# A delta-rule recurrence on one core: the identity added at the eviction of W, X and Y copied out whole, four quadrants of the array in use

## What is computed

```python
def step(state, inp):                       # per head: 16 heads of 64 channels
    r_t, w_t, k_t, v_t, a_t, b_t = inp
    sa = jnp.einsum('bhvk,bhk->bhv', state, a_t)
    state = (state * w_t[:, :, None, :]
             + sa[:, :, :, None] * b_t[:, :, None, :]
             + v_t[:, :, :, None] * k_t[:, :, None, :])
    y_t = jnp.einsum('bhvk,bhk->bhv', state, r_t)
    return state, y_t
...
y_f = _wkv7_scan(r32, decay_h[0], k_dir[0], v32, -kk, b_dir[0], reverse=False)
y_b = _wkv7_scan(r32, decay_h[1], k_dir[1], v32, -kk, b_dir[1], reverse=True)
```

## Time and profile before

| | before |
|---|---|
| median of 3 executions | 2935.41 us |
| lowest and highest | 2929.65, 2935.97 us |
| span of the profiled execution | 2930.1 us |
| TensorE (PE) busy in it | 2793.3 us, 95% |
| VectorE (DVE) busy | 2161.7 us, 74% |
| ScalarE (ACT) busy | 1632.9 us, 56% |
| GpSimd (POOL) busy | 159.4 us, 5% |
| stretch with levels | about 173.6 to 445.6 us |

### The profile page before, as it was taken

One profiled execution on the slowest core, in us unless ns is written; L12 is line 12 of the kernel. 1 busy time (PEld: TensorE's weight loads), 2 busy tenths in 40 slices (PEclk: granted clock), 3 DMA queues, 4 the chain that ended last, 5 costly groups with the idle time before them and its releaser, 6 DMA issues.

```text
span 2930.1 us, 52775 instructions
## 1 busy us (share of the span) xinstructions
PE 2793.3 (95%) x21826; PEld 2485.1 (85%) x21826; DVE 2161.7 (74%) x2714; ACT 1632.9 (56%) x2317; POOL 159.4 (5%) x164
## 2 busy tenths in 40 slices
PE   6889999999999999999999999999999999999999
PEld 5877777778778999878787888999999979998998
DVE  7868875899996656689998666666666786668665
ACT  2445543788884444478888544445544824446443
POOL 0024430000000020100000000000000000000000
PEclk8989999999999999999999999999999999999999
DMA  7601124699995736179998413554455404544453
GB/s 318 237 2 46 60 74 155 232 354 350 356 354 192 273 132 243 44 288 353 356 357 339 187 58 118 185 186 147 155 186 187 157 12 177 186 159 142 148 185 129
DMA packets 78260, 572.73 MB, mean 195 GB/s; under 512 B 8802, under 2 KB 8930, under 8 KB 9186
## 3 DMA queue, kind: packets, MB, share of 16 engines
q1 hardware_dynamic: 76752, 558.93, 51.3%
q10 hardware_dynamic: 1298, 10.83, 0.9%
HBM read 568.67 MB, written 1.05 MB: 194 GB/s over the span
## 4 chain that ended last, share of the span: by engine, by line
PE 82%; DVE 12%; ACT 3%; DMA 1%; issue 1%; POOL 0%; DVEq 0%; SPq 0%; ACTq 0%; PEldq 0%
PE ps L1377 14%; PE ps L1299 13%; PE ps L1254 8%; PE ps L1398 7%; PE ps L863 5%; PE ps L865 5%; PE ps L864 5%; PE ps L1255 4%; DVE arena L2245 4%; DVE wl L2239 2%; DVE arena L2239 2%; PE ps L1497 1%; DMA ring<-in_stream 1%; PE ps L898 1%; PE ps L897 1%; PE ps L896 1%
## 5 line engine op out<-in xcount | busy, mean ns | idle before, releaser
L2239 DVE TENSOR_TENSOR wl<-ring,wh 128x1024 fp32r<-128x1024 f32 (+1 forms) x560 | 938.2, 1695 | 366.1 <-ACT wh L1636 345.6
L1636 ACT ACTIVATE wh<-ring 128x1024 fp32r<-128x1024 f32 (+1 forms) x560 | 789.5, 1432 | 454.4 <-PE ps L1255 209.6
L1254 PE MATMUL ps<-hx,wh 128*128 128x512 f32 x1024 | 362.4, 396 | 1.3 <-DVE wl L2239 1.3
L863 PE MATMUL ps<-hx,wh 128*128 128x256 f32 x1072 | 310.6, 290 | 22.5 <-DVE hx L2239 17.4
L864 PE MATMUL ps<-hx,wl 128*128 128x256 f32 x1072 | 306.5, 286 | 0.0
L865 PE MATMUL ps<-hx,wh 128*128 128x256 f32 x1072 | 306.3, 286 | 0.0
L1299 PE MATMUL ps<-hidh,wh 128*128 128x256 f32 x1024 | 290.4, 284 | 1.1 <-DVE hidl L2239 1.1
L1299 PE MATMUL ps<-hidl,wh 128*128 128x256 f32 x1024 | 289.8, 283 | 0.0
L1299 PE MATMUL ps<-hidh,wl 128*128 128x256 f32 x1024 | 289.7, 283 | 0.0
L1255 PE MATMUL ps<-hx,wl 128*128 128x256 f32 x1024 | 287.1, 280 | 0.0
L1633 ACT ACTIVATE arena<-arena 128x256 f32<-128x256 f32 (+7 forms) x420 | 207.2, 498 | 97.5 <-DVEq L2766 33.8
(11 more groups left out here) (286 smaller groups left out, 5662.0 us busy)
## 6 DMA issues: line engine op xcount, KB each, us to landing
ring<-in_stream SPq DMA_DIRECT2D x532, 1024.0 KB, 4.9
arena<-in_wcmp ACTq DMA_DIRECT2D x2, 2048.0 KB, 10.5
arena<-in_lora ACTq DMA_DIRECT2D x1, 2048.0 KB, 9.8
arena<-in_atm ACTq DMA_DIRECT2D x1, 1762.0 KB, 11.6
x<-in_xT ACTq DMA_DIRECT2D x1, 1024.0 KB
out<-x SPq DMA_DIRECT2D x1, 1024.0 KB, 3.9
arena<-in_rwm ACTq DMA_DIRECT2D x1, 736.0 KB, 12.8
cols<-in_cols ACTq DMA_DIRECT2D x1, 715.0 KB
```

Source lines behind the costliest of these rows:

```text
L863: mm(out, w[0], h[0], start=first, stop=False)
L1254: mm(o.rearrange("p (a s) -> p a s", a=2), w[0], hx[:, :, k, :], start=k == 0, stop=False, skip_group_check=True)
L1636: return nc.scalar.activation(out, in_, ACT.Copy)
L2239: return v.tensor_tensor(out, a, b, op)
```

## The change

**Algebra.** With Y = X', the sum X + Y'W is Y'(W + I), and Y + W'Y is (W + I)'Y. VectorE now evicts W with the identity added, as 256 columns for each `z`. The products of `level_xy` are then the new X and Y themselves, and ScalarE copies them out, 512 columns from two PSUM banks for each `z` (256 from one bank in level 5). The two engines have changed places in each level.

**Quadrants.** `y_half` says in which half Y and W lie: in their own at level 1, in the other one from level 2 on. X stays in its half. So the product for X and that for Y use different quadrants, and the four products of one `q` (X and Y, both halves) are written one behind another.

**PSUM.** W and X of a `z` share bank 2z, Y takes bank 2z + 1. W of level 1 therefore waits now until X of level 5 of the block before has been copied out.

**Order.** The evictions of the levels are moved on both engines, as is P0 on ScalarE. TensorE's order outside `level_xy`, and GpSimd's, are the same.

```diff
+        def y_half(lev, i):
+            return HALF[i if lev == 1 else 1 - i]
...
 def level_w(c, lev):                                  # TensorE
                         if lev == 1:
                             pe.wait_ge(ev("rw_x0"), c + 1)
+                            if c:
+                                pe.wait_ge(ev("rw_xy"), rw_at(c - 1, RW_LEVELS, z))
                         else:
                             pe.wait_ge(ev("rw_xy"), rw_at(c, lev - 1, z))
-                        t, A_ = ps[:, z, :], Al[(RW_LEVELS * c + lev - 1) % 3]
+                        t, A_ = ps[:, 2 * z, :], Al[(RW_LEVELS * c + lev - 1) % 3]
                         for q in range(4):
-                            for r in HALF:
-                                last = mm(t[r, 64 * q:64 * q + 64], A_[r, z, 64 * q:64 * q + 64], XY[c % 3][r, z, 0, 64 * q:64 * q + 64],
-                                          start=True, stop=True)
+                            a = slice(64 * q, 64 * q + 64)
+                            for i in (0, 1):
+                                last = mm(t[y_half(lev, i), a], A_[HALF[i], z, a], XY[c % 3][HALF[i], z, 0, a], start=True, stop=True)
...
 def level_xy(c, lev):                                 # TensorE
-                            for r in HALF:
-                                last = mm(t[r, a], XY[c % 3][r, z, 1, a], Wb[r, z, a], start=True, stop=True)
-                        if lev < RW_LEVELS:
-                            for q in range(4):
-                                a = slice(64 * q, 64 * q + 64)
-                                for r in HALF:
-                                    last = mm(t[r, 256 + 64 * q:320 + 64 * q], Wb[r, z, a], XY[c % 3][r, z, 1, a], start=True, stop=True)
+                            for i in (0, 1):
+                                h = y_half(lev, i)
+                                last = mm(ps[HALF[i], 2 * z, a], XY[c % 3][h, z, 1, a], Wb[h, z, a], start=True, stop=True)
+                            if lev < RW_LEVELS:
+                                for i in (0, 1):
+                                    h = y_half(lev, i)
+                                    last = mm(ps[HALF[1 - i], 2 * z + 1, a], Wb[h, z, a], XY[c % 3][h, z, 1, a], start=True, stop=True)
...
 def level(c, lev):                                    # ScalarE
-                        act.wait_ge(ev("rw_Wt"), rw_at(c, lev, z))
-                        copy(Wb[:, z, :], ps[:, z, 0:256]).then_inc(ev("rw_w"), 1)
+                        act.wait_ge(ev("rw_XYt"), rw_at(c, lev, z))
+                        if lev < RW_LEVELS:
+                            copy(XY[c % 3][:, z], ps[:, 2 * z:2 * z + 2, 0:256]).then_inc(ev("rw_xy"), 1)
+                        else:
+                            copy(XY[c % 3][:, z, 0, :], ps[:, 2 * z, 0:256]).then_inc(ev("rw_xy"), 1)
...
 def level(c, lev):                                    # VectorE
-                        dve.wait_ge(ev("rw_XYt"), rw_at(c, lev, z))
-                        a = XY[c % 3][:, z].rearrange("p x n -> p (x n)")[:, 0:512 if lev < RW_LEVELS else 256]
-                        tt(a, ps[:, 2 + z, 0:512 if lev < RW_LEVELS else 256], a, ADD).then_inc(ev("rw_xy"), 1)
+                        dve.wait_ge(ev("rw_Wt"), rw_at(c, lev, z))
+                        tt(Wb[:, z, :].rearrange("p (q t) -> p q t", q=4), ps[:, 2 * z, 0:256].rearrange("p (q t) -> p q t", q=4),
+                           rmask("eye")[:, None, :].to_broadcast([P, 4, 64]), ADD).then_inc(ev("rw_w"), 1)
```

More of the change, by code:

```diff
@@ L1758, in rwkv @@
                     on_e, on_f, on_c, on_p, on_g = e < C, 0 <= f < C, 0 <= c < C, 0 <= p < C, 0 <= g < C
+                    if on_p:
+                        solved("P", 0, p)
                     if on_c:
                         level(c, 1)
-                    if on_p:
-                        solved("P", 0, p)
                     if on_f:
@@ L1770, in rwkv @@
                         fn(cx, cx, ACT.Exp).then_inc(ev("rw_E"), 1)
-                    if on_c:
-                        level(c, 2)
                     if on_p:
@@ L1776, in rwkv @@
                         let(copy(Zv[c % 2], got("Zv", c)), "Zv", c)
+                        level(c, 2)
                     if on_p:
@@ L1787, in rwkv @@
                         let(copy(Vt[f % 3].rearrange("p j n -> p (j n)"), got("V", f)[:, 0:S]), "V", f)
-                    if on_c:
-                        level(c, 3)
                     if on_f:
@@ L1792, in rwkv @@
                             copy(Ast[f % 2][:, h].rearrange("p z j t -> p (z j t)"), got(f"sm{h}", f)[:, 0:256]).then_inc(ev("rw_A"), 1)
+                    if on_c:
+                        level(c, 3)
                     if on_g:
@@ L1818, in rwkv @@
                             let(copy(N6[f % 2][:, h].rearrange("p j t -> p (j t)"), got(f"n6{h}", f)[:, 0:P]), f"n6{h}", f)
-                    if on_c:
-                        level(c, 5)
                     if on_e:
@@ L1837, in rwkv @@
                         let(copy(ys, got("y", p)), "y", p)
+                    if on_c:
+                        level(c, 5)
                     if s == C:
@@ L2471, in rwkv @@
                     on_e, on_f, on_c, on_p, on_g = e < C, 0 <= f < C, 0 <= c < C, 0 <= p < C, 0 <= g < C
+                    if on_c:
+                        level(c, 1)
                     if on_f:
@@ L2486, in rwkv @@
                         modulation("ada1")
-                    if on_c:
-                        level(c, 1)
                     if on_p:
                         solved_r(p, 0)
+                    if on_c:
+                        level(c, 2)
                     if on_g:
@@ L2533, in rwkv @@
                         tt(X4, X4, rmask("eye")[:, None, None, :].to_broadcast([P, 2, 4, 64]), ADD).then_inc(ev("rw_x0"), 1)
+                    if on_c:
+                        level(c, 4)
                     if on_p:
@@ L2538, in rwkv @@
                             masked(Arb[f % 3], "rb", h, f, "incl")
-                    if on_c:
-                        level(c, 4)
                     if on_e:
```

3 lines of the change are left out of this document (removed).

## The result

The changed kernel takes 2914.5 us (median of 8 runs, 2900.2 to 2916.4), the kernel before on the same chip 2932.9: a ratio of 0.9935, interval 0.992 to 0.9949. Timed once more on the chip of the last experiments, it is 2905.1 against 2930.4: 0.9916 (0.9894 to 0.9938). So it is faster by 18 to 25 us. Forecast were 2919 and a range of 2903 to 2932, which holds both medians; but several terms of the sum were off, in opposite directions, as the profile shows.

The account below looks back on a forecast made before the run. Neither PE nor DVE alone was the bound: a step's first half is a DVE chain, its second mostly PE. Gains of 6 x 1.8 + 3 + 2.5 = 16.3 us from 2935.4 gave 2919 us, range 2903 to 2932.

Parts of the forecast that it names:

- step 0: First step, without U0: its 2.44 us wait before W of level 2 goes entirely, gaining about 3 us.
- steps 1 to 6: Six recurrence steps, each 34.3 instead of 36.1 us: 1.8 us less per step.
- step 7, to X of level 5: Last step, where DVE idles: PE's shorter products count, less some eviction waits, gaining 2.5 of 3.4 us.
- from there to the next stage: Stretch behind the last step's levels: no gain of its own in the sum; the next stage starts 16.3 us earlier.
- the walk: One step followed through PE, DVE and ACT in the new order: 34.3 instead of 36.1 us.
- the wait before W of level 2: PE's 0.97 us for late X and Y of level 1: mostly gone, but U0 then waits for R0; gain 0.4.
- the gain up to `sm`: First half of a step, on DVE: features at 12.6, `sm` at 12.75 us against 14.25, gain 1.5.
- R1 waits on ACT: P1's copy queues on ACT until 19.75, R1 starts at 19.9; half the gain is given back, 1.0 us left.
- four quadrants are no faster than two: Rival on X and Y products: a level stays at 2.0 us, total 2935 us; chance 0.13.
- The rival of a late ACT: A copy over two PSUM banks costs ACT 1.2 us, W of level 5 comes 1.55 later: 2947 us; chance 0.06.
- The rival of better meshing: DVE and PE mesh better, no waits at U0 and R1; halfway 3.5 us a step, 2907 us; chance 0.10.
- the price of the evictions: DVE's W plus identity costs 0.89 us a pair against 1.28 for X and Y: 1.55 us less DVE a step.

Follow-up runs that it names:

- changed, again: The changed kernel unchanged, in a second profiled execution (span 2904.5 us) and timed once more: 2905.1 us, ratio 0.9916 to the kernel before.
- P1 early: Changed kernel, but on ScalarE var's Exp and the squares of k moved behind BK and P1: 2911.7 us, ratio 0.9927 to the kernel before.
- busy_tail: Changed kernel plus overwritten filler products ahead of TensorE's waits at R and U from step 7 on and S and Z1 behind the last step: 2912.2 us.
- R0 early: Changed kernel, but on VectorE R0 is evicted directly behind the scans, ahead of what follows from them: 2903.3 us, ratio 0.9898 to the kernel before.
- the kernel in pairs: Changed kernel, but Y and W stay in their own half, so X and Y use the same two quadrants: 2921.5 us, ratio 0.9967 to the kernel before.
- the kernel before, again: The kernel before, unchanged, run once more for a second profile: 2945.5 us in one execution.

## Why the prediction was right, and where it was not

**The whole.** By stretches, from W of level 1 of step 0 to the stage behind the recurrence, against the profile of before:

| stretch, us | before | changed | changed, again | forecast gain | gain, changed and again |
|---|---|---|---|---|---|
| step 0 | 32.5 | 23.6 | 23.6 | 3 | 8.9 |
| steps 1 to 6 | 213.4 | 199.3 | 193.6 | 10.8 | 14.1, 19.8 |
| step 7, to X of level 5 | 25.1 | 26.1 | 23.4 | 2.5 | -1.0, 1.7 |
| from there to the next stage | 37.2 | 42.4 | 41.4 | 0 | -5.2, -4.2 |

It comes to 16.9 and 26.2 us, against 16.3. So the closeness to the first result is partly luck: steps 0 to 6 gained more than was forecast, and low clock, with stalls, took it back: 4.2 us behind the recurrence in both executions, and in the first 5.6 more in the steps, 2.7 in step 7 and 1.0 behind it. The tail's part is not shown to be the change's doing: the kernel before has 37.2 and 42.4 there in its two profiles, and other kernels with the change have 38.6 ("P1 early") to 42.8 (`busy_tail`).

**Right: the mechanisms of the walk.** Four quadrants do a level in 1.0 us (forecast 1.09); the wait before W of level 2 is gone, and U0 waits for R0 in its place; the gain up to `sm` is fixed by DVE (R0 early); R1 waits on ACT, whose queue holds P1 (P1 early), and gives back part. The wait of W of level 1 for X of level 5 costs nothing. But P1, forecast to come after a wait of about 1 us, hardly waits (without the block it starts only 0.15 earlier).

**The rivals.** That four quadrants are no faster than two is out: both halves of X write one bank, both of Y another, and a pair of X and one of Y together take the 58 ns that one pair took before. The Trainium skill, "TensorEngine Tiling (Array Packing)", section "Gotcha 1: PSUM Pressure", says that different row tiles cannot access the same PSUM bank simultaneously; in this pattern the trace shows nothing of it. That rival was also priced too high, 2935 with W of level 5 at 26.8: the kernel in pairs, which has just these products, has it at 26.15 and takes 2921.5. The rival of a late ACT is out: the pair of copies over two banks took 1.09, where it needed 1.8 to decide. The rival of better meshing, given 0.10, had the size: "some 3.5 a step" and 2907, where 3.2 and, in the second timing, 2905.1 were measured. Its mechanism did not come true, since it put the waits at U0 and R1 at nothing and they are there (0.80 and 1.34); what made the step shorter is the next point.

**Mis-sized: the price of the evictions.** The walk took 0.89 for a pair of W from a pair at the end of a wait. Queued behind other work a pair takes 0.74 (298.12, 302.21), and five of them are 0.75 less. A single eviction is about as long in both places (0.42 and 0.41): at 310.16 the second begins 0.47 after the first, since it still waits for PE, and in the queue 0.33 after. So 0.89 held a wait that the new place does not have. The block of 2048 columns, with 3.06 the dearest single term, took 2.41 here. That is more than scatter: the block at this place took 3.06 or 3.07 in steps 2 to 6 of both profiles of the kernel before, and 2.40 to 2.42 in steps 2 to 6 of "changed, again" and in steps 4 to 6 of the first profile of the changed kernel (2.90 and 2.52 in steps 2 and 3, which have low clock). Over all of the recurrence its mean went only from 2.73 to 2.60 (busy us and mean ns of one, before and then changed), since the step's other block went from 2.70 to 2.80. In step 7 and behind it, where GpSimd is idle, each block takes 2.34 or 2.35 in both kernels. Why the same instruction takes longer elsewhere was not tested. In all, DVE is busy 3.4 us less in a step, and the walk had 1.55.

```profile
L2245 DVE SCALAR_TENSOR_TENSOR ring<-ring,small 128x2048 f32<-128x2048 f32 x14 | 38.2, 2730 | 0.9 <-DVE under L2242 0.3 <-DVE spare L2245 0.3
```

```profile
L2250 DVE SCALAR_TENSOR_TENSOR ring<-ring,small 128x2048 f32<-128x2048 f32 x14 | 36.4, 2599 | 0.3 <-DVE spare L2250 0.3
```

Both lie on DVE's chain to P1, which comes at 16.2 and not 17.6: three pairs (0.45) and the block (0.65) are 1.1 of these 1.4 us. The remaining 0.3 I can't assign. The step is shorter than forecast by 1.4 too, 32.9 and not 34.3, but not by this alone. At W of level 5 only 1.0 of it is left (23.8 against 24.75). Another 0.4 comes behind it, where the walk said that nothing changes: `ka` and `kr` took 2.37 until the next W in the kernel before (310.51 to 312.88) and take 1.99 in "changed, again" (323.71 to 325.70).

```profile
310.51 2.45 PE L1235 MATMUL ps<-arena,under 64*128 64x128 f32 x32
```

```profile
323.71 2.06 PE L1238 MATMUL ps<-arena,under 64*128 64x128 f32 x32
```

**Wrong: step 0.** The forecast of 3 came from the wait of 2.44 us alone. What it did not see are the records right behind it: Zv at 180.52 took 3.19 us, against 2.00 in the step from 276.78, and X of level 2 1.12 for 16 records, against 0.68. The window of that stretch of the kernel before comes first (12 us at 0.72), then the whole step 0 of the changed kernel, at 1.00:

```profile
178.00:190.00 12.00, 9.71 (x146) 8.95 (x146) 7.23 (x13) 4.13 (x9) 0.00 (x0) 0.72 0.01 2
```

```profile
172.59:196.20 23.61, 21.05 (x612) 18.08 (x611) 19.18 (x38) 14.58 (x33) 11.33 (x14) 1.00 0.02 4
```

The same 612 records take 28.2 us of PE before and 21.1 after, of which the quadrants explain 3.6 (in pairs it is 24.6). A wait was costed by its length, without the slower records that follow it. The kernel in pairs has 25.7 for step 0 and clock 1.00, so hands and order bring 6.8 of the 8.9 us. Both profiles of the kernel before have the wait of 2.44 and a clock of 0.89 in step 0, and all eleven of kernels with DVE's new order have 1.00 there, so this gain is no chance of one execution. Step 1 has some of it too, since the kernel before has low clock there (34.6 us at 0.95, in "changed, again" 29.35 at 1.00).

**Wrong: the clock in the other steps.** Nothing in the forecast spoke of it, since the earlier trace rows say 1.00. In the first profile of the changed kernel, 2 us of step 3 look so:

```profile
270.00:272.00 2.00, 2.00 (x64) 1.88 (x56) 1.97 (x5) 1.20 (x2) 0.00 (x0) 0.50 0.00 0
```

```profile
269.23 0.37 PE L1030 MATMUL ps<-under,arena 64*64 64x64 f32 x2
269.25 0.37 PE L1034 MATMUL ps<-arena,under 64*64 64x64 f32 x2
269.39 0.32 PE L1030 MATMUL ps<-under,arena 64*64 64x64 f32 x2
```

The granted clock is 0.50, the lower of the two levels (1.2 GHz), with PE busy the whole time, and a level takes 1.9 us instead of 1.0 (269.23 until 271.15), as much as it took on two quadrants. Ahead of it stands the wait of U0. "Changed, again" has the same wait in each step and whole clock behind it. So the wait alone does not decide, and why the one execution has it and the other not stays open. The runs of the changed kernel spread accordingly, from 2900 to 2918 us, by mean clocks of 0.984 to 0.976.

**Step 7.** At whole clock it is 1.7 us shorter (25.14 to 23.40), where 2.5 was forecast. But the 23.40 hold a stall of 0.96 us (the last section) that the 25.14 do not; without it the gain would be about 2.7, an estimate from these two numbers, and so the forecast stands. In the first profile a longer stall and low clock behind it hide the gain.

## What to carry to other kernels

Where an operand can lie in the other partition half, four small products at once cost half of two at once, and here the two halves could share a PSUM bank; but the engine that evicts the operation in the middle of a level must come to it in time: with the same products and VectorE's old order the kernel was 0.7% slower, with the new one 0.6 to 0.8% faster. Cost a wait on TensorE by its length and by the records behind it: look at the granted clock of the stretch that follows. And before a stretch of one profile is compared with one of another, profile both kernels twice: here the same work took 37.2 and 42.4 us in two executions of one program.

## What was not expected of the hardware

TensorE stalls in the middle of a run of W, in both kernels, with nothing that the profile shows for it. The first row is of the changed kernel's step 7, the second of the kernel before, again, also in step 7:

```profile
415.12 0.97 PE L1020 MATMUL ps<-arena 64*64 64x64 f32 x25 [2.11 <-issue]
```

```profile
442.46 1.24 PE L1013 MATMUL ps<-arena 64*64 64x64 f32 x32 [2.73 <-issue]
```

In the 5 us behind each of them the granted clock is 0.66. Shorter ones, of 0.3 to 1.3 us, occur in other steps, and "changed, again" has one of 0.96 at the same W of level 5 and takes 23.4 us for step 7 instead of 26.1. No stall of this kind is in step 7 of the first profile of before.

They belong to a place in TensorE's program, not to a moment. The number of matmul records from the start of the trace to the stall in step 7 is the same, 6365, in all six profiles of kernels without added products and with DVE's new order, though the stall ends anywhere between 404.9 and 426.4 us. The windows up to it, of the changed kernel and of "changed, again" (length, busy PE with records, clock, DMA):

```profile
0.00:415.11 415.11, 343.12 (x6365) 0.93 0.35 130
```

```profile
0.00:409.31 409.31, 340.02 (x6365) 0.95 0.35 132
```

Its length varies from 0.96 to 2.60 us. Behind those of 2.11 and 2.60 and that of 2.73 of the kernel before the clock fell (0.66 in 5 us), behind those of 0.96 to 1.48 it did not (1.00). So a stall of this kind is one way in which two executions of one program come to differ. What causes it is open.
